# A two-layer decoder trunk on one core: x turned by token halves, and the last 328 attention columns taken as rounded parts

## What is computed

```python
for i in range(DEPTH):
    p = x @ (w_in0 if i == 0 else w_in_rest[i - 1])
    p_att = p[..., :N_ATT]                                  # 584 columns: 256 + 128 + 128 + 64 + 8
    p_gate = p[..., N_ATT:N_ATT + N_GATE]                   # 2048 columns
    p_rw = token_shift(p[..., N_ATT + N_GATE:N_IN0], mu_rwkv[i])
    cq_raw, k_raw, v_raw, ik_raw, iw_raw = split_cols(p_att, ATT_SIZES)
    y_a = dsa_sparse_mqa(cq_raw, k_raw, v_raw, ik_raw, iw_raw, ...)
    ...
    y_b = rwkv7_time_mix(pr, pk, v, pw, pa, pg, ...)
    x = layer_norm(alpha * x + (g_a * y_a + g_b * y_b) @ w_out[i], ln1_g[i], ln1_b[i])
    x = layer_norm(alpha * x + conv_glu_ffn(x, ...), ln2_g[i], ln2_b[i])
```

## Time and profile before

| | us |
|---|---|
| median of 3 runs | 1148.6 (1147.91 to 1149.32) |
| the profiled execution | 1147.24 |
| its span, first to last instruction | 1145.2 |
| TensorE busy | 1113.5 (97%) |
| VectorE busy | 809.0 (71%) |
| ScalarE busy | 556.7 (49%) |

### The profile page before, as it was taken

One profiled execution on the slowest core, in us unless ns is written; L12 is line 12 of the kernel. 1 busy time (PEld: TensorE's weight loads), 2 busy tenths in 40 slices (PEclk: granted clock), 3 DMA queues, 4 the chain that ended last, 5 costly groups with the idle time before them and its releaser, 6 DMA issues.

```text
span 1145.2 us, 29677 instructions
## 1 busy us (share of the span) xinstructions
PE 1113.5 (97%) x12504; PEld 1010.6 (88%) x12504; DVE 809.0 (71%) x1473; ACT 556.7 (49%) x960; POOL 54.5 (5%) x49
## 2 busy tenths in 40 slices
PE   7999999999999999999999999999999999999997
PEld 7978888888898899998798888888888988999985
DVE  2578776877576887774545886868685778877745
ACT  2544554545454565553235445545453545555531
POOL 0000000000000100000100000000000000000001
PEclk9999999999999999999999999999999999999999
DMA  8433122222365465566464322222223745555651
GB/s 291 155 106 118 61 100 75 85 75 86 127 242 183 167 199 188 185 197 198 135 218 141 117 89 88 76 86 84 77 76 123 263 149 184 196 191 187 203 194 60
DMA packets 45514, 165.41 MB, mean 144 GB/s; under 512 B 5168, under 2 KB 5424, under 8 KB 45136
## 3 DMA queue, kind: packets, MB, share of 16 engines
q1 hardware_dynamic: 42736, 154.03, 40.2%
q0 software_dynamic: 1504, 7.47, 2.2%
q10 hardware_dynamic: 1152, 2.10, 0.6%
HBM read 160.44 MB, written 3.15 MB: 143 GB/s over the span
## 4 chain that ended last, share of the span: by engine, by line
PE 86%; DVE 7%; ACT 2%; POOL 1%; issue 1%; DMA 1%; DVEq 0%; SPq 0%; ACTq 0%; POOLq 0%
PE ps L735 21%; PE ps L736 19%; PE ps L737 19%; PE ps L886 10%; PE ps L710 4%; PE ps L1044 3%; PE ps L1088 1%; PE ps L1104 1%; POOL g L673 1%; DVE ring_r L1608 1%; PE ps L898 1%; PE ps L787 1%; PE ps L828 1%; PE ps L847 1%; PE ps L815 1%
## 5 line engine op out<-in xcount | busy, mean ns | idle before, releaser
L735 PE MATMUL ps<-x_tok_r,mid_hi 128*128 128x256 f32 x576 | 175.6, 305 | 1.5 <-issue 1.0
L736 PE MATMUL ps<-yb_hi,mid_hi 128*128 128x256 f32 x576 | 162.3, 282 | 0.5 <-issue 0.5
L737 PE MATMUL ps<-x_tok_r,ring_r 128*128 128x256 f32 x576 | 162.2, 282 | 0.0
L735 PEld LDWEIGHTS ps<-x_tok_r,mid_hi 128*128 128x128 f32 x576 | 108.6, 189 | 10.5 <-issue 3.4
L1229 ACT CAST mid_hi<-ring 128x1024 fp32r<-128x1024 f32 x80 | 83.8, 1047 | 60.0 <-PE ps L737 45.4
L736 PEld LDWEIGHTS ps<-yb_hi,mid_hi 128*128 128x128 f32 x576 | 108.9, 189 | 2.6 <-issue 2.6
L1608 DVE TENSOR_TENSOR ring_r<-ring,mid_hi 128x1024 fp32r<-128x1024 f32 x80 | 96.8, 1210 | 19.7 <-ACT mid_hi L1229 19.5
L737 PEld LDWEIGHTS ps<-x_tok_r,ring_r 128*128 128x128 f32 x576 | 108.9, 189 | 0.0
L1856 DVE TENSOR_TENSOR rs_ks_r<-ring,tha_kkn_r 128x1024 fp32r<-128x1024 f32 x44 | 53.9, 1224 | 20.7 <-ACT tha_kkn_r L1271 20.7
L1856 DVE TENSOR_TENSOR w_lo<-ring,w_hi 128x1024 fp32r<-128x1024 f32 x42 | 51.4, 1224 | 21.2 <-ACT w_hi L1271 21.1
L1856 DVE TENSOR_TENSOR X_Y_r<-ring,arc_r 128x1024 fp32r<-128x1024 f32 x42 | 51.3, 1221 | 21.3 <-ACT arc_r L1271 21.2
(11 more groups left out here) (452 smaller groups left out, 3332.8 us busy)
## 6 DMA issues: line engine op xcount, KB each, us to landing
ring<-stream_dram SPq DMA_DIRECT2D x281, 512.0 KB, 3.5
lora_w<-lora_dram POOLq DMA_DIRECT2D x2, 1536.0 KB, 7.5
W_bt<-rpar_dram POOLq DMA_DIRECT2D x4, 512.0 KB, 5.1
kt_V<-rpar_dram POOLq DMA_DIRECT2D x4, 512.0 KB, 6.8
x_tok<-x_dram SPq DMA_DIRECT2D x2, 512.0 KB, 4.8
v_saved_dram<-vs_dC ACTq DMA_DIRECT2D x4, 256.0 KB, 4.1
x_tok<-x_dram SPq DMA_DIRECT2D x1, 1024.0 KB, 5.2
vf<-v_saved_dram ACTq DMA_DIRECT2D x4, 256.0 KB, 3.4
```

What stands on the lines that cost most here:

```text
L735: pe.matmul(dst, lh, rh, start=start, stop=False)
L736: pe.matmul(dst, lh, rl, start=False, stop=False)
L737: return pe.matmul(dst, ll, rh, start=False, stop=stop)
```

## The change

Four things change at the head of both layers.

1. x is turned by halves. TensorE turns half t=0, multiplies it with attention slots 0 and 1 in full precision, then turns half t=1 and does the same for it. ScalarE empties all four quarters of the first half and quarters 0 and 2 of the second, VectorE quarters 1 and 3 of the second. There is a semaphore for each x half's load and each half's save. VectorE writes x's half t once half t is turned.
2. The last 328 attention columns (584 - 256) are computed as products of rounded parts, 328 columns wide, with x as the stationary side, into PSUM banks 4 and 5: 3 matmuls x 8 inner blocks x 2 halves. Attention slots 2, 3 and 4 join `MIDS` for this (`ATT_MIDS = 3`), before lora 0.
3. For these products a slot holds three inner blocks (the third slot two) of all 328 columns. The stream in DRAM is as before, so SP fetches such a slot with three transfers, of 128, 128 and 72 columns, out of the three old slots (`rest`). `landed_by(n)` counts 48 instead of 16 for such a slot.
4. x is rounded in two casts and two subtractions, `xr0` and `xr1`, of four inner blocks each. In layer 1 `xr0` waits for the save of x's first half, `xr1` for that of the second. The angle tables and `dpar` come after the three attention subtractions on VectorE, and ScalarE's sines after the cast of lora 0. The copy of the attention columns out of PSUM is split: the first 256 (`pq`) once slot 1 is used, with their squares, and the rest later.

```diff
-MIDS = [... or s[1] == "oa" and s[2] < 2 * OA_EARLY or s[1] == "lora" ...]
+MIDS = [... or s[1] == "oa" and s[2] < 2 * OA_EARLY or s[1] == "att" and s[2] >= 2 or s[1] == "lora" ...]
+ATT_MIDS = 3
-FIRST_MIDS = 2 + 3 * GB
+FIRST_MIDS = ATT_MIDS + 2 + 3 * GB
...
 SP
+            def rest(n):
+                i, k = rest_of(n), n % RING
+                a, nk = 3 * i, min(3, KB - 3 * i)
+                dst = ring[:, k, 0:nk * N_REST].rearrange("p (b c) -> p b c", c=N_REST)
+                for c in range(3):
+                    w = min(P, N_REST - c * P)
+                    src = stream[n - i + c].rearrange("p (b c) -> p b c", c=P)
+                    sp.dma_start(dst[:, :, c * P:c * P + w], src[:, a:a + nk, 0:w]).then_inc(landed[k], 16)
...
 TensorE
-            pe.wait_ge(x_in_sbuf, 16 * 3)
             for l in L2:
-                transposed_x(l, "T")
-                for c in range(5):
+                turned_half(l, "T", 0)
+                def att_half(c, t):
                     w = slot(l, "att", c)
-                    n = min(P, N_ATT - c * P)
-                    for t in range(TT):
-                        dst = bank(2 + t)[:, c * P:c * P + n] if c < 4 else bank(4)[:, t * P:t * P + n]
-                        for kb in range(KB):
-                            if c == 0 and t == 0 and kb % 2 == 0:
-                                pe.wait_ge(*(dve_xT if kb // 2 % 2 else act_x)(l, f"T{kb // 2}"))
-                            mm = pe.matmul(dst, xT[:, kb, t * P:t * P + P], w[:, kb * P:kb * P + n],
-                                           start=(kb == 0), stop=(kb == KB - 1))
+                    dst = bank(2 + t)[:, c * P:c * P + P]
+                    for kb in range(KB):
+                        if c == 0 and kb % 2 == 0:
+                            by_dve = t and kb // 2 % 2
+                            pe.wait_ge(*(dve_xT if by_dve else act_x)(l, f"T{t}{kb // 2}"))
+                        mm = pe.matmul(dst, xT[:, kb, t * P:t * P + P], w[:, kb * P:kb * P + P],
+                                       start=(kb == 0), stop=(kb == KB - 1))
...
+                for c in range(2):
+                    att_half(c, 0)
+                turned_half(l, "T", 1)
+                for c in range(2):
+                    att_half(c, 1)
+                for i in range(ATT_MIDS):
+                    m = MID_AT[l, "att", 2 + i] % MID_PER_LAYER
+                    pe.wait_ge(*dve_mid(l, m))
+                    hi, lo = mid_hi[m % NM], rounded["ring"][:, SLOT_AT[l, "att", 2 + i] % RING, :]
+                    for kb in range(3 * i, min(3 * i + 3, KB)):
+                        if kb in (0, 4):
+                            pe.wait_ge(*dve_parts(l, f"xr{kb // 4}"))
+                        c = slice(kb % 3 * N_REST, kb % 3 * N_REST + N_REST)
+                        for t in range(TT):
+                            left = xr_hi[:, kb * T + t * P:kb * T + t * P + P], xr_lo[kb // 4][:, kb % 4, t * P:t * P + P]
+                            mm = product(bank(4 + t)[:, 0:N_REST], left, (hi[:, c], lo[:, c]), kb == 0, kb == KB - 1)
                     mm.then_inc(slot_used, 1)
...
 ScalarE
-                xT_out(l, "T")
+                if l:
+                    mids_up_to(l, NM)
+                xT_out(l)
+                for j in range(2):
+                    if l:
+                        act.wait_ge(x_saved[j], 16)
+                    act.wait_ge(*act_x(l, f"T1{2 * j}"))
+                    act.wait_ge(*dve_xT(l, f"T1{2 * j + 1}"))
+                    act.copy(xr_hi[:, 4 * T * j:4 * T * j + 4 * T], blocks(xT, 4 * j, 4)).then_inc(*act_parts.inc(l, f"xr{j}"))
...
-                if l:
-                    act.wait_ge(x_saved, 16 * TT)
-                act.wait_ge(*act_x(l, "T2"))
-                act.wait_ge(*dve_xT(l, "T3"))
-                act.copy(xr_hi, flat(xT)).then_inc(*act_parts.inc(l, "xr"))
...
 VectorE
                     elif l + 1 < DEPTH:
-                        dve.wait_ge(*pe_x(l + 1, f"T{0 if t == 0 else 3}"))
+                        dve.wait_ge(*pe_x(l + 1, f"T{t}3"))
...
             for l in L2:
+                for j in range(2):
+                    if l:
+                        mids_up_to(l, j + 1)
+                    dve.wait_ge(*act_parts(l, f"xr{j}"))
+                    dve.tensor_tensor(xr_lo[j]..., blocks(xT, 4 * j, 4), f32(xr_hi[...]), ALU.subtract)
+                mids_up_to(l, ATT_MIDS)
+                if l == 0:
+                    angles()
...
-                dve.wait_ge(*act_parts(l, "xr"))
-                for j in range(2):
-                    last = dve.tensor_tensor(xr_lo[j]..., blocks(xT, 4 * j, 4), f32(xr_hi[...]), ALU.subtract)
-                last.then_inc(*dve_parts.inc(l, "xr"))
-                mids_up_to(l, NM)
+                mids_up_to(l, ATT_MIDS + 2)
```

More of the change, by code:

```diff
@@ L60 @@
 N_ATT = D_CQ + 2 * DH_A + D_IDX + H_IDX
+N_REST = N_ATT - D_CQ
 N_GATE = 2 * D
@@ L409, in trunk @@
         stored = sem("stored")
-        x_saved = sem("x_saved")
+        x_saved = [sem(f"x_saved{t}") for t in range(TT)]
         x_back = sem("x_back")
@@ L417, in trunk, with rest_of, width, landed_by @@
         tables = sem("tables")
+        def rest_of(n):
+            l, kind, i = SLOTS[n]
+            return i - 2 if kind == "att" and i >= 2 else None
+        def width(n):
+            i = rest_of(n)
+            return D if i is None else min(3, KB - 3 * i) * N_REST
+        def landed_by(n):
+            return sum(16 if rest_of(m) is None else 48 for m in range(n % RING, n + 1, RING))
         def used(l, kind, i):
@@ L567, in refill @@
                 sp.wait_ge(wait, value)
+                if isinstance(n, int) and rest_of(n) is not None:
+                    rest(n)
+                    return
                 src = stream[n] if isinstance(n, int) else stream[bass.ds(n, 1)].rearrange("a p d -> p (a d)")
@@ L591, in _ @@
                 end = n + 1
-                while end < len(SLOTS) and (SLOTS[end - RING] in SPLIT_AT) == split and end not in between:
+                while (end < len(SLOTS) and (SLOTS[end - RING] in SPLIT_AT) == split and end not in between
+                       and rest_of(end) is None and rest_of(n) is None):
                     end += 1
```

218 lines of the change are left out of this document (122 added, 96 removed).

## The result

| | before | after |
|---|---|---|
| median, us | 1147.9 (13 runs) | 1150.99 (13 runs) |
| ratio | 1 | 1.0024 (95% interval 1.0016 to 1.0031) |
| profiled execution, us | 1147.24 | 1150.43 |
| its span, us | 1145.2 | 1148.3 |
| TensorE's mean granted clock | 0.997 | 0.990 |

The change makes the kernel 0.24% slower, 2.8 us. I had forecast no difference; the time lies within my range of 1145.3 to 1152, but I had put slower than before at a chance of 0.27.

What follows compares the result with a forecast made beforehand. TensorE, busy 97% of the span, was taken to bound the kernel. Layer 0's +1.0 us and layer 1's -1.05 summed to 0 on the profiled 1147.24 us, giving a forecast median of 1148.5 us, range 1145.3 to 1152.

Steps and rivals of the forecast that it cites:

- TensorE's work: Both layers' heads: 96 records removed, 48 products 328 wide added at 0.152 us each, saving 3.4 us a layer.
- Layer 0: Layer 0's head: waits for part 4 and VectorE's order put lora's first product 1.0 us later, at 30.2 us.
- my third wait: Layer 0, before the third product group: TensorE waits 1.35 us for attention part 4's landing, cast and subtraction.
- the mark: Start of lora's first rounded products in each layer: 29.15 and 591.59 us before, forecast 30.2 and 590.55.
- Layer 1: Layer 1's head: a new 4.3 us wait for x's save, yet lora's first product 1.05 us earlier, at 590.55.
- A page against the rows: Weighed the skill's rule that idle TensorE falls to 1.2 GHz against a row reading 1.00 after 7.9 idle us.
- rival D: Layer 1: granted clock at half level after the wait, 18 products 2.7 us slower in all; 1151.2 us, chance 0.06.
- B: Rival: transfers are not late, part 4 lands at 22 us in layer 0; 1145.7 us, chance 0.28.
- C: Rival: finely cut slots are dear, delaying lora transfer and part 4 in layer 0; 1151.9 us or more, chance 0.21.
- My sign that the end must move by the sum of the two marks' shifts: Whole kernel: an end shift differing from both marks' summed shifts would mean something later in the layers answers too.

Runs made afterwards that it cites:

- e9: The changed kernel with angle tables and derived parameters ahead of part 4's subtraction, and layer 1's lora_w and kirow loaded in layer 0; 1143.36 us, 0.9955 of before.
- e16: Turning by halves and two-step rounding of x only, all five attention slots whole in full precision, layer 1's lora_w loaded early; 0.9977 of before.
- e1: The changed kernel with 17 filler matmuls on TensorE in layer 1 ahead of the first 328-wide product; 1.0032 of before.
- e7: The changed kernel with angle tables moved ahead of part 4's subtraction and 17 filler matmuls before layer 1's first 328-wide product; 1150.47 us, 1.0014 of before.
- e2: The changed kernel with 8 filler matmuls on TensorE in layer 0 ahead of lora's first product; 1.0051 of before.
- e3: The changed kernel with angle tables and derived parameters on VectorE ahead of attention part 4's subtraction; 1.0013 of before.
- e5: The changed kernel with layer 1's lora_w load issued only after both copies of x have landed; 1.0000 of before.
- e13: The kernel with angles moved and lora_w early, plus a deliberate TensorE wait in layer 1 for eight GpSimd pow operations; 1.0019 of before.
- e15: The kernel with angles moved and lora_w early, plus 24 products of zeros on TensorE at the kernel's start; 0.9956 of before.
- e14: The kernel with angles moved, lora_w early and a deliberate wait for eight pow operations, plus 16 filler products ahead of that wait; 1.0018 of before.
- e10: The kernel before, with only layer 1's lora_w and kirow loaded early, at about 380 us; 0.9996 of before.
- e11_gap: The kernel with angles moved and lora_w early, plus a deliberate TensorE wait in layer 1 for three GpSimd pow operations; 0.9976 of before.

## Why the prediction was wrong, step by step

- **TensorE's work.** Products 0.150 us apart, 0.152 predicted. The pace is right. Of the 6.8 us that I had them save over both layers, e9 against e16 shows 1.7 in the stage, 2.2 at layer 0's transposes and 2.5 in the time.
- **Layer 0.** Slot 0 came at 8.8 (9.15 predicted). The 32 records of the first blocks took 5.4 us instead of 3.56, from the cold start, and the second turning 0.93 instead of 1.74; the products began at 19.94 (19.2), with 1.0 of waiting (1.2). lora_w was issued at 14.00 us, 0.7 later than before where I had 1.1 to 1.5: the small packets were as cheap as the earlier trace rows said. Part 4's cast ran at 23.73 (24.4), its subtraction was done before it was needed, and my third wait (1.35) was not there. Angles, `dpar` and lora 0's subtraction stand behind it as predicted, and the mark is 29.49 (30.2). So the mark is 0.7 us sooner than forecast, with luck in it: the slow blocks at the start and the missing third wait nearly cancel.
- **Layer 1.** Shifted by layer 0's 1.09 us, I had the cast at 581.5, the first product at 583.8 behind a wait of 4.3, and the mark at 591.6. They came at 581.22, 583.67, 4.38, and 594.39. Everything up to the first product is right within 0.3 us; the mark is 2.75 late, and 2.5 of that is 20 products at 0.273 instead of 0.150.
- **The step that failed is the one under "A page against the rows"**, and rival D with it: "clock 1.00 after 7.9 idle us", so a chance of 0.06, and nothing for it in the sum. The clock fell behind both new waits, 1.4 us of product time in layer 0 and 2.5 in layer 1. For layer 1 that is rival D's mechanism and nearly its price (18 products at twice the time, 2.7 us). That its 1151.2 is so near the 1150.99 is partly luck, since D had no fall in layer 0 and my layer 0 was 0.7 us too late. Taken off the marks, the fall accounts for the miss: a stage of 26.00 - 2.5 = 23.5 would be 0.8 us under before, where I had 1.05. In the whole time no run shows this, since e1 and e7 kept the clock at 1.00 and were no faster. The Trainium skill ("TensorE: Matmul & The Clock Gate", Part 1: The HAM clock gate) says that an idle TensorE drops to 1.2 GHz. The traces agree: 0.50 behind the long waits of after, e2, e3, e5 and e13 (4.0 to 6.0 us).
- **Why the row misled.** At the start the granted clock's row reads 1.00 whatever the pace is: e15 and after both read 1.00 from 10 to 14 us and did 38 and 28 instructions. The pace would have told. The earlier trace rows has 16 records of turning in 3.63 us at the start of the kernel, and the earlier trace rows 16 records of the same shape in 2.05 in layer 1. Both rows stood in front of me; I even took the second turned half (1.74) from the slow one.
- **Rivals B and C.** Part 4's cast ran at 23.73, between B's 22 and my 24.4, and lora_w was issued only 0.7 us later than before. C's dear packets did not come.
- My sign that the end must move by the sum of the two marks' shifts failed: the mark of layer 0 moved by 0.34, and that of layer 1, counted from its first turned block as in my working, by 1.71. The sum is 2.05, and the span moved by 3.1. Layer 0's 1.4 us of slow products came behind its mark, and only about 0.8 us of the lateness was absorbed later.

What is shown: that a wait without work can drop the clock and that work in it holds it, by e1 and e2 against after, and by e13 and e14; that lora_w's transfer makes layer 1's wait, by e5 and e9, and that taking it away turns the loss into a gain, by e9 against e3; that the early load gives before nothing, by e10. Not shown is that the clock alone costs its 1.7 to 2.5 us in the whole time, since fillers gave none of it back; and what layer 0's wait costs in the whole time is not clear of noise (e3).

## What to carry to other kernels

Price a new wait of TensorE at its length and, as a case of its own with a good chance, at the work behind it done at half speed (1.4 to 2.5 us more on the timeline here, behind waits of 2.04 and 4.38 us). Look for a way to let the wait vanish before you fill it. Read the clock from the pace of equal instructions, not from its row alone. And where a change makes TensorE wait for a transfer, look what large transfer is issued just ahead of it and has no reader for long: here 1.5 MB wanted 70 us later made 0.58% of the time, the most of the way from 0.24% slower to 0.45% faster.

## What the runs showed of the hardware that I had not expected

- The same wait held the clock in one run and dropped it in another. Before and e10_before_lora_w_early have the same wait at 571 us, 2.08 and 2.07 us; in the first the stretch 572 to 573 has 11 instructions at 1.00, in the second 6 at 0.50:

```profile
572.00:573.00 1.00, 1.00 (x11) 1.00 (x10) 0.79 (x1) 0.84 (x3) 0.05 (x1) 1.00 1.03 184
```

```profile
572.00:573.00 1.00, 1.00 (x6) 1.00 (x6) 0.00 (x0) 0.09 (x1) 0.00 (x0) 0.50 0.00 0
```

  2.04 us dropped it in after's layer 0, 2.50 held it in e11_gap. For e10 that is a stage of 25.35 us instead of 24.29.
- Three pow operations on GpSimd, 1.55 us each when alone, took 2.37 us together, and eight took 5.90.
